# A two-layer hybrid decoder trunk on one core: the even layer's step reordered on four engines

## What is computed

```python
p = h @ even_w_in                      # qa, ka, va (attention) and r, k, v, wl, al, gl (RWKV-7)
a_out = diff_attention(qa, ka, va)     # 8 heads, two score maps of 64 dims each, causal
b_out = rwkv7_time_mix(...)            # 16 heads of 64, delta-rule state, data-dependent decay
x = x + concat(a_out, b_out) @ even_w_out
```

## Time and profile before

| what | before |
|---|---|
| runs | 2721.53, 2723.00, 2723.12 us, median 2723.0 |
| profiled execution | 2722.15 us |
| its span, first to last instruction | 2720.4 us |
| TensorE busy | 2599.1 us, 96% |
| VectorE busy | 1932.7 us, 71% |
| ACT busy | 1267.0 us, 47% |
| POOL busy | 439.2 us, 16% |
| mean granted TensorE clock | 0.985 |
| chain that ended last | TensorE 87%, VectorE 7%, issue 3%, ACT 2% |

### The profile page before, as it was taken

One profiled execution on the slowest core, in us unless ns is written; L12 is line 12 of the kernel. 1 busy time (PEld: TensorE's weight loads), 2 busy tenths in 40 slices (PEclk: granted clock), 3 DMA queues, 4 the chain that ended last, 5 costly groups with the idle time before them and its releaser, 6 DMA issues.

```text
span 2720.4 us, 47053 instructions
## 1 busy us (share of the span) xinstructions
PE 2599.1 (96%) x16642; PEld 2261.5 (83%) x16642; DVE 1932.7 (71%) x2973; ACT 1267.0 (47%) x1719; POOL 439.2 (16%) x426
## 2 busy tenths in 40 slices
PE   7988888869999999999999999998999999999998
PEld 6777777758888888888888888887888888888886
DVE  6676666757666566656698999997766656665666
ACT  5444343435555344434465565554455434433444
POOL 1222222211111011101111212111111001100112
PEclk9999999969999999999999999999999999999999
DMA  6222222205455555555554444443545555555543
GB/s 252 96 101 95 81 99 90 95 32 185 170 187 190 194 185 185 188 191 189 177 182 172 168 155 166 154 158 134 190 170 187 197 187 185 185 189 189 192 161 134
DMA packets 65568, 437.83 MB, mean 161 GB/s; under 512 B 9408, under 2 KB 10816, under 8 KB 15936
## 3 DMA queue, kind: packets, MB, share of 16 engines
q1 hardware_dynamic: 61632, 435.84, 45.6%
q10 hardware_dynamic: 3840, 0.70, 0.1%
HBM read 434.41 MB, written 2.10 MB: 160 GB/s over the span
## 4 chain that ended last, share of the span: by engine, by line
PE 87%; DVE 7%; issue 3%; ACT 2%; DMA 0%; POOL 0%; DVEq 0%; ACTq 0%; SPq 0%; POOLq 0%
PE acc L337 52%; PE acc L342 27%; PE mixer_banks L1490 2%; DVE w_low L307 1%; PE mixer_banks L1225 1%; PE mixer_banks L1309 1%; PE mixer_banks L1322 1%; PE acc L319 1%; ACT w_high L302 1%; DVE arena L358 0%; PE mixer_banks L1324 0%; ACT arena L626 0%; DVE arena L939 0%; DVE arena L927 0%; DMA w_raw<-w_even 0%
## 5 line engine op out<-in xcount | busy, mean ns | idle before, releaser
L307 DVE TENSOR_TENSOR w_low<-w_raw,w_high 128x1024 fp32r<-128x1024 f32 x836 | 1053.0, 1261 | 425.7 <-ACT w_high L302 415.2
L302 ACT ACTIVATE w_high<-w_raw 128x1024 fp32r<-128x1024 f32 x836 | 882.0, 1059 | 981.4 <-PE acc L342 963.8
L337 PE MATMUL acc<-h_split,w_high 128*128 128x512 f32 x4576 | 1194.3, 398 | 8.5 <-DVE arena L358 8.1
L337 PEld LDWEIGHTS acc<-h_split,w_high 128*128 128x128 f32 x4576 | 816.9, 189 | 161.4 <-issue 18.9
L342 PEld LDWEIGHTS acc<-h_split,w_low 128*128 128x128 f32 x4576 | 641.3, 190 | 55.7
L342 PE MATMUL acc<-h_split,w_low 128*128 128x256 f32 x4576 | 659.2, 282 | 0.0
L451 POOL TENSOR_TENSOR arena<-arena,norm_scale 128x256 f32<-128x256 f32 x202 | 222.1, 1100 | 1787.5 <-DVE arena L358 1786.3
L337 PE MATMUL acc<-mix_split,w_high 128*128 128x512 f32 x1888 | 479.9, 395 | 3.3 <-DVE mix_split L1023 2.7
L337 PEld LDWEIGHTS acc<-mix_split,w_high 128*128 128x128 f32 x1888 | 340.6, 190 | 64.6 <-issue 4.1
L342 PEld LDWEIGHTS acc<-mix_split,w_low 128*128 128x128 f32 x1888 | 260.8, 191 | 20.3
L342 PE MATMUL acc<-mix_split,w_low 128*128 128x256 f32 x1888 | 266.6, 283 | 0.0
(11 more groups left out here) (246 smaller groups left out, 1650.4 us busy)
## 6 DMA issues: line engine op xcount, KB each, us to landing
w_raw<-w_gu SPq DMA_DIRECT2D x176, 1024.0 KB, 4.8
w_raw<-w_down SPq DMA_DIRECT2D x64, 1024.0 KB, 4.9
w_raw<-w_odd SPq DMA_DIRECT2D x64, 1024.0 KB, 4.8
w_raw<-w_even SPq DMA_DIRECT2D x50, 1024.0 KB, 4.9
w_raw<-w_down SPq DMA_DIRECT2D x32, 768.0 KB, 4.2
w_raw<-w_even_out SPq DMA_DIRECT2D x16, 1024.0 KB, 4.8
w_raw<-w_odd_out SPq DMA_DIRECT2D x16, 1024.0 KB, 4.8
x_residual<-xT SPq DMA_DIRECT2D x4, 512.0 KB, 9.5
```

Source lines behind the costliest of these rows:

```text
L302: act.activation(wh[:, self.res, ks], raw[:, self.raw, ks], ACT.Copy).then_inc(high_done, 1)
L307: dve.tensor_tensor(wl[:, self.res, ks], raw[:, self.raw, ks], wh[:, self.res, ks].bitcast(F32), ALU.subtract).then_inc(low_done, 1)
L337: pe.matmul(acc[self.acc][:, 0:2 * T], wh[:, self.res, k], flat(split[:, k]), start=k == 0, stop=k == self.kt - 1)
```

## The change

Five moves, all in the even layer's step; no arithmetic is added or left out.

1. ACT: the square of the key stands ahead of the table load and of high(3).
2. ACT: the loads of `gu` and `pln` for step j are issued in step j itself, after high(5), and no longer at the end of step j - 1 ahead of high(2).
3. VectorE: the token shift of step j + 1 stands in step j behind low(13), ahead of the last products. It waits for the bonus (`rw_bv`) where it waited for the end of the step (`rw_end`).
4. TensorE, ACT: z(l) writes bank 1 in place of bank 2, and z(1) no longer waits for KTR. VectorE: KTR stands behind the maxima of the attention's scores, and level 1 behind it, ahead of evacuate(1) and low(7). The wait for KTR stands ahead of its first reader, `rw_R0`.
5. TensorE: the attention's scores stand behind the next three tiles.

```diff
@@ ACT, even_step
                 act.activation(ag, bank(0)[:, 0:T], ACT.Sigmoid, bias=pj[:, P_A0:P_A0 + 1]).then_inc(S["rw_a"], 1)
-                act.preload_act_table_set("natural_log_exp_and_others")
-
-                high(3)
                 act.wait_ge(S["rw_xv"], j + 1)
                 act.activation(d3[:, 2], xm[:, 1], ACT.Square, scale=pj[:, P_KK:P_KK + 1]).then_inc(S["rw_sq"], 1)
+                act.preload_act_table_set("natural_log_exp_and_others")
+                high(3)
...
                 high(5)
+                if not isinstance(j, int) or j > 0:
+                    waits(act, j, "rw_yTs", "rw_g")
+                    act.dma_start(gu[0:32], g_up[j]).then_inc(S["rw_late"], 16)
+                    act.dma_start(pln, par_ln[j]).then_inc(S["rw_late"], 16)
...
-                    act.activation(flat(Zs)[rows], bank(2)[rows, 0:256], ACT.Copy).then_inc(S["rw_Zs"], 1)
+                    act.activation(flat(Zs)[rows], bank(1)[rows, 0:256], ACT.Copy).then_inc(S["rw_Zs"], 1)
...
-                if more:
-                    waits(act, j + 1, "rw_yTs", "rw_g")
-                    act.dma_start(gu[0:32], g_up[j + 1]).then_inc(S["rw_late"], 16)
-                    act.dma_start(pln, par_ln[j + 1]).then_inc(S["rw_late"], 16)
@@ VectorE
+            def token_shift(j):
+
+                dve.wait_ge(S["even_scaled"], 6 * j + 5)
+                if not isinstance(j, int) or j > 0:
+                    dve.wait_ge(S["rw_bv"], j)
+                dve.wait_ge(S["rw_par"], 32 * j + 32)
+                dve.tensor_scalar(omka, pj[:, P_KA:P_KA + 1], -1.0, 1.0, ALU.mult, ALU.add).then_inc(S["rw_prep"], 1)
+                dve.tensor_tensor(d3, r3[:, :, 0:T], r3[:, :, 1:], ALU.subtract).then_inc(S["rw_prep"], 1)
+                dve.wait_ge(S["rw_prep"], 9 * j + 2)
+                for c, name in ((1, "rw_xk"), (0, "rw_xr"), (2, "rw_xv")):
+                    dve.scalar_tensor_tensor(xm[:, c], d3[:, c], pj[:, P_MU + c:P_MU + c + 1], r3[:, c, 1:],
+                                             ALU.mult, ALU.add).then_inc(S[name], 1)
...
-                dve.wait_ge(S["even_scaled"], 6 * j + 5)
-                dve.wait_ge(S["rw_end"], j + 1)
-                dve.wait_ge(S["rw_par"], 32 * j + 32)
-                dve.tensor_scalar(omka, pj[:, P_KA:P_KA + 1], -1.0, 1.0, ALU.mult, ALU.add).then_inc(S["rw_prep"], 1)
-                dve.tensor_tensor(d3, r3[:, :, 0:T], r3[:, :, 1:], ALU.subtract).then_inc(S["rw_prep"], 1)
-                dve.wait_ge(S["rw_prep"], 9 * j + 2)
-                for c, name in ((1, "rw_xk"), (0, "rw_xr"), (2, "rw_xv")):
-                    dve.scalar_tensor_tensor(xm[:, c], d3[:, c], pj[:, P_MU + c:P_MU + c + 1], r3[:, c, 1:],
-                                             ALU.mult, ALU.add).then_inc(S[name], 1)
...
-                dve.wait_ge(S["rw_m2"], j + 1)
-                for n in range(2):
-                    dve.tensor_tensor(KTR[:, 2 * n:2 * n + 2], bank(2 + n).rearrange("p (a b) -> p a b", a=2), tri, ALU.mult).then_inc(S["rw_KTR"], 1)
...
                 dve.tensor_scalar(anb, amx, -0.125, None, ALU.mult).then_inc(S["at_nb"], 1)
+                dve.wait_ge(S["rw_m2"], j + 1)
+                for n in range(2):
+                    dve.tensor_tensor(KTR[:, 2 * n:2 * n + 2], bank(2 + n).rearrange("p (a b) -> p a b", a=2), tri, ALU.mult).then_inc(S["rw_KTR"], 1)
+                level(1)
                 evacuate(1)
                 low(7)
-                level(1)
                 low(8)
...
                 low(13)
+                if more:
+                    token_shift(j + 1)
                 waits(dve, j + 1, "rw_yTs", "rw_bv")
...
+            token_shift(0)
             even_step(0, even_block(0))
@@ TensorE, even_step
                 last.then_inc(S["rw_m2"], 1)
                 dense(3)
-                pe.wait_ge(S["rw_T0"], 3 * j + 2)
-                waits(pe, j + 1, "at_qk")
-                for c in range(2):
-                    rows = slice(64 * c, 64 * c + 64)
-                    pe.matmul(bank(4 + c)[:, 0:P], qk[rows, 0, 0:P], qk[rows, 1, 0:P], start=True, stop=True)
-                    last = pe.matmul(bank(4 + c)[:, P:3 * P], qk[rows, 0, P:T], qk[rows, 1], start=True, stop=True)
-                last.then_inc(S["at_s"], 1)
...
-                            last = pe.matmul(bank(2)[64:P, 64 * n:64 * n + 64], LTR[0:64, n, 64:P], TT[0:64, n, 0], start=True, stop=True)
+                            last = pe.matmul(bank(1)[64:P, 64 * n:64 * n + 64], LTR[0:64, n, 64:P], TT[0:64, n, 0], start=True, stop=True)
...
-                    if l == 1:
-                        pe.wait_ge(S["rw_KTR"], 2 * j + 2)
...
-                            last = pe.matmul(bank(2)[r, 64 * n:64 * n + 64], Xb[r, l % 2, n], TT[r, n, 0], start=True, stop=True)
+                            last = pe.matmul(bank(1)[r, 64 * n:64 * n + 64], Xb[r, l % 2, n], TT[r, n, 0], start=True, stop=True)
...
                 dense(3)
+                pe.wait_ge(S["rw_T0"], 3 * j + 2)
+                waits(pe, j + 1, "at_qk")
+                for c in range(2):
+                    rows = slice(64 * c, 64 * c + 64)
+                    pe.matmul(bank(4 + c)[:, 0:P], qk[rows, 0, 0:P], qk[rows, 1, 0:P], start=True, stop=True)
+                    last = pe.matmul(bank(4 + c)[:, P:3 * P], qk[rows, 0, P:T], qk[rows, 1], start=True, stop=True)
+                last.then_inc(S["at_s"], 1)
                 z(1)
...
                 z(6)
+                waits(pe, 2 * j + 2, "rw_KTR")
                 pe.wait_ge(S["rw_kbn"], j + 1)
```

More of the change, by code:

```diff
@@ L582, in even_step @@
                 act.activation(ag, bank(0)[:, 0:T], ACT.Sigmoid, bias=pj[:, P_A0:P_A0 + 1]).then_inc(S["rw_a"], 1)
+                act.wait_ge(S["rw_xv"], j + 1)
+                act.activation(d3[:, 2], xm[:, 1], ACT.Square, scale=pj[:, P_KK:P_KK + 1]).then_inc(S["rw_sq"], 1)
                 act.preload_act_table_set("natural_log_exp_and_others")
                 high(3)
-                act.wait_ge(S["rw_xv"], j + 1)
-                act.activation(d3[:, 2], xm[:, 1], ACT.Square, scale=pj[:, P_KK:P_KK + 1]).then_inc(S["rw_sq"], 1)
                 act.wait_ge(S["rw_b"], 2 * j + 2)
```

## The result

The changed kernel takes 2728.1 us (median of 14 runs, 2726.0 to 2729.9), the kernel before 2722.6 us in the same session (2720.8 to 2724.7). The ratio is 1.0021 with a 95% interval of 1.0013 to 1.0029: slower by 0.21%, on the very edge of what a measurement of this kernel tells from no change. The profiled execution takes 2729.85 us, 7.7 more than that of before; it is one of the slowest of the fourteen.

The account below looks back on a forecast made before the run. VectorE was taken to set the pace up to L976, TensorE from there to y. From 2722.15 us, -1.5 + 4.3 - 1.2 - 4.6 + 3.4 = +0.4 gives 2722.6, plus 0.85 for the median 2723.4 us; range 2711 to 2733.

Parts of the forecast that it names:

- the forecast's case: Whole kernel: the sum of the terms with 0 to 4 clock falls, 2720 to 2727 us; chance 0.45.
- the clock falls in most steps (slower): TensorE behind its wait for L976: 5 or more clock falls, seven giving 2732 to 2738 us; chance 0.27.
- token shift: VectorE, shift ahead of the last products: idle gaps filled, less a hold; 0.3 us in five steps, -1.5 us.
- KTR later, holds: VectorE up to L976: POOL's operations hold low(6), low(8) and L973; +0.6 us in steps 0 to 6, +4.3 us.
- step 7: Last step, no weights split: no such hold, and KTR leaves the path to the exponentials; -1.2 us.
- loop ends: VectorE's standstill at the jump in steps 3 and 5 shrinks from 4.54 to 2.2 us; -4.6 us.
- TensorE's clock: TensorE idles 2.3 us before the transposes; 2 clock falls in 7 steps at 1.7 us each, +3.4 us.
- VectorE paces up to L976, TensorE from there to y: Each step: VectorE sets the pace from readout y to L976, TensorE to the next y; edits count by VectorE's queue.
- The gap before L1258 will go and come back at L1269: TensorE, square moved ahead: the 1.35 us wait before L1258 goes, but TensorE then waits at L1269; price 0.
- no holds: VectorE's low(6) and low(8): POOL's operations don't get in between and no clock falls; -11.1 us, 2712 us; chance 0.22.
- "wrong" sign: VectorE at the loop's jump: a standstill still of 4.5 us would show the prediction wrong.
- Waits are TensorE's own: TensorE before L1258: if VectorE had hidden slack, the waits are won whole, 20 us, 2703 us; chance 0.06.

Follow-up runs that it names:

- e9: Changed kernel with low(8) behind level(2) and the token shift back at the head of its step: 2716.5 us.
- e4: Changed kernel with low(8) moved behind level(2), ahead of evacuate(2), on VectorE: 2712.6 us.
- e1: Changed kernel with KTR and level 1 back at their earlier places in VectorE's queue, Z still in bank 1: 2722.9 us.
- e3: Changed kernel with the four tiles that follow the transposes of the attention weights put ahead of them: 2713.2 us.
- e8: Kernel before the change with only low(8) moved behind level(2): 2718.4 us.
- e10: e7 with the square back behind the table load and the high half: 2696.5 us.
- e5: Changed kernel with VectorE's loop over steps 1 to 6 written out as six steps: 2721.3 us.
- e2: Kernel before with only the new place of KTR and level 1, Z in bank 1 and the moved wait for KTR: 2731.6 us.
- e12: e7 with KTR and level 1 back at their earlier places on VectorE, Z still in bank 1: 2711.8 us.
- e11: e7 with the attention scores three tiles earlier, as before the change: 2695.4 us.
- e7: Changed kernel with the edits of e3, e4 and e5 together: 2696.6 us.
- e13: e7 with the three tiles that follow z(2) put ahead of it: 2694.1 us.

## Why the prediction came out as it did

The time forecast, 2723.4 us, is 4.7 below what was measured. That lies inside the range, and at the edge between the forecast's case and the first rival, "the clock falls in most steps (slower)", which had the chance 0.27. The mechanism is that rival's: it was to decide from 5 falls on, and 5 came. Against the profiled execution, from which its terms were read, the sum is off by 7.3 us; the medians bring it nearer mainly because that execution of the changed kernel is a slow one, 1.7 above its median, which is luck.

| term | forecast | measured |
|---|---|---|
| token shift | -1.5 | -2.5 (0.41 in six steps, e9 against e4) |
| KTR later, holds | +4.3 | +4.2 (0.60 in seven steps, changed against e1) |
| step 7 | -1.2 | -2.5, not separable from the clock |
| loop ends | -4.6 | -1.2 |
| TensorE's clock | +3.4 (2 x 1.7) | +7.2 (5 x 1.45) |
| elsewhere in this execution | 0 | +2.1 |
| sum against the profiled execution | +0.4 | +7.3, measured +7.7 |

- *VectorE paces up to L976, TensorE from there to y.* Right, and e3, e4 and e8 rest on it. "The gap before L1258 will go and come back at L1269" was right in kind: L1262 waits for nothing in steps 1 to 6, while 1.20 and 0.53 us stand before the products for evacuate(-1) and L1273. In e10 the square's place is worth 0.00 us per step.
- *Holds.* Low(6) at 1.66 us (1.65 forecast), low(7) and low(8) together 2.79, L974 longer by 0.33 (0.34 charged), TensorE's wait 2.31 (2.3 forecast). With KTR back (e1) low(6) is at 1.21. The "no holds" rival (0.22) is excluded. The Trainium skill, SBUF — State Buffer, section Who interferes with whom, lets tensor_scalar block against GpSimd; L974 at 0.88 and e4's L973 at 1.28 agree with it. Two slips of the working: 7 x 0.6 is 4.2, where the prediction has 4.3, and the rows of VectorE in step 1 that it cites as rows 4 (L911, L939, L970 and L976 among them) stand in rows 5, those of the token shift in rows 4.
- *Loop ends.* This step failed: "I take the standstill at 2.2 us then, nearest to the 1.9". I had put the length of the standstill down to weights that pass beside it, from the landing times of two small loads. With 4 GB/s beside it the jump still costs 3.9 us, in two stops. My "wrong" sign, a standstill still of 4.5, was too coarse to catch the second stop; the time between readouts, 4.5 longer in a step with a loop end before and 3.9 now, says it directly. The Trainium skill, Runtime: NRT & Kernel Launch, section Instruction fetch mechanics, says that a jump outside the pages held forces a fetch; e5 agrees that the stop is the jump's (both stops and seven instruction packets go with it), and that page did not support my -4.6, only that there is a stop.
- *Clock.* This step failed: "I take 2 falls in 7 steps". The mechanism, the place, the wait's length and nearly the price (1.45 for 1.7) were right; the frequency was read from three single gaps elsewhere in the trace. Over five kernels (changed, e2, e5, e1, e12), waits of 2.2 to 2.3 us in this stretch were followed by a fall in 23 of 31 cases (5 of 7, 5 of 6, 4 of 5, 5 of 7, 4 of 6), waits of 1.35 to 1.45 us in 1 of 27 (before, changed, e1, e2), and those of 1.13 and less before the transposes in none of 28 (before, e3, e4, e9). Short waits are not safe everywhere, though: over steps 0 to 6 of all fourteen kernels, before the scores, z(1) and other readers, 2 of 51 waits of 1.25 to 1.6 us and 3 of 125 of 1.0 to 1.25 us were followed by a fall. Step 0 of e5:

```profile
89.29 0.68 PE L1302 MATMUL mixer_banks<-arena 64*64 64x64 f32 x16 [1.07 <-DVE arena L937]
89.90 0.96 PE L337 MATMUL acc<-h_split,w_high 128*128 128x512 f32 x2
90.66 0.63 PE L342 MATMUL acc<-h_split,w_low 128*128 128x256 f32 x2
```

  The two products take 0.96 us where they take 0.73 at the full clock, and the granted clock is 0.50 from 91 to 93 us. What decides between equal waits stays open.
- *Step 7* can't be read. The changed kernel and e4 have the same code there and take 55.0 and 51.4 us; the clock held in the one and not in the other. The windows of the stretch ahead of y, of the changed kernel and of e4:

```profile
599.00:603.00 4.00, 3.63 (x16) 3.12 (x15) 0.49 (x2) 0.28 (x1) 0.00 (x0) 0.50 0.00 0
```

```profile
579.00:583.00 4.00, 3.27 (x25) 2.66 (x24) 0.42 (x1) 0.56 (x2) 0.00 (x0) 1.00 0.00 0
```

  The 2.1 us outside the even layer lie in code that neither kernel has changed; I did not settle their cause. At one wait of equal length both traces differ, 2.51 us for eight products behind it now, with a granted clock of 0.50 just after, against 2.09.
- *Waits are TensorE's own* (0.06) is excluded by e10 and e11.

The likeliest case was thus taken wrongly by two terms of about 3.5 us each, both toward "faster"; the token shift and step 7 took some of it back.

## What to carry to other kernels

Where one engine paces the first part of a step and TensorE the second, a longer wait between them costs twice: its length, and often a fall of the clock behind it (here a fall in three of four waits of 2.2 to 2.3 us, at 1.0 to 1.5 us each, and none at 1.13 in the same place). A fall costs only where TensorE sets the pace. Move work that is ready into such a wait first: four tiles moved won 15 us on the changed kernel, which had lost 5.5. To price an edit of tenths of a microsecond, first make a version whose steps repeat, and read it from the time between two readouts rather than from medians of a few runs: single runs of one kernel lie up to 6.6 us apart here, and a step 7 with and without a fall 3.6.

## What the runs showed of the hardware that I had not expected

- A jump back on VectorE costs about 4 us with no other traffic, in two stops: 2.78 us and, ending 2.3 us after the first, another 1.09. Where the code behind the jump stands as before it is one stop of 4.5 us (4.2 and 3.9 in e9). Without the jump neither is there.
- Equal waits have both outcomes for the clock: before the transposes it was kept in 4 of 18 waits of 2.3 us, and lost in both of 1.81 (e5) but not in the one of 1.72 (e2). In all three of these the clock had fallen once already earlier in the step and had come back.
- The spread of a kernel's runs does not follow its long waits: 2696.5 to 2698.0 us in e7's four runs, but 2690.6 to 2696.3 in e13's four and 2708.7 to 2714.8 in e4's five, neither with a fall behind the waits of the table; 2726.0 to 2729.9 in the changed kernel's fourteen.
- POOL's operation that is released during a VectorE operation goes in ahead of the next one in VectorE's own queue: both holds are of that kind, 0.44 us each (1.66 - 1.22, and 2.79 - 2.35). This is read from order and length: POOL's scaling takes 1.55 us when it starts beside low(7) and 0.64 alone, and low(8) is the one that is long.
